# First loads in another order, fourteen transposes ahead of the first product, and a last norm made token tile by token tile, in a two-block model on one core

## The chip, the cores and the metric

One of the cores of a Trainium2 chip runs the whole program. The metric is the device time of one execution in microseconds. Five engines run beside each other, each through a queue of its own in order: TensorE (PE, with its weight loads as PEld), VectorE (DVE), ScalarE (ACT), GpSimd (POOL) and SyncE (SP), which here only issues transfers.

## The reference

`x` holds 256 tokens of 1024 channels. Three kinds of stages follow each other, all with a residual: feed-forwards, an even mixer (convolution and banded attention), an odd mixer (dilated attention and pooling) and two mixers of a second block. The change touches the first feed-forward, the last feed-forward and the last norm:

```python
def rms_norm(x, g):
    y = x * rsqrt(mean(x * x, axis=-1, keepdims=True) + EPS)
    return y * g
def swiglu(x, w_gate, w_up, w_down):
    return (silu(x @ w_gate) * (x @ w_up)) @ w_down

x = x + 0.5 * swiglu(rms_norm(x, g[0]), ffn_w_gate[0, 0], ...)     # first stage, 2752 hidden channels
...
x = x + swiglu(rms_norm(x, ffn_norm_g_2[1]), w_ffn_gate_2[1], ...) # last stage, 2816 hidden channels
return rms_norm(x, final_norm_g_2)
```

## The kernel before

The residual stream `xs` stays in SBUF as two token tiles `t` of 128 tokens by 1024 channels. Weights arrive in units of 128x1024 fp32 (512 KB), listed in `plan` in the order in which they are used. SyncE loads unit `u` into the stage `u % 6`; ScalarE's `split` copies it, rounded, to `whi[u % 4]`; VectorE's `split` writes the rest, `wlo = stage - whi`. TensorE then makes every fp32 product from two or three products of such halves (`three`). The unit's `whi`/`wlo` are free once TensorE has signalled `("used", u)`, four units back.

All queues are written out by hand. `Count` gives each step a semaphore and a value: `K.at(step)` waits for a step, `K.now(name)` for the last increment of one's own. `Banks` hands out the eight PSUM banks, and `room` waits until the bank's earlier user has been read.

A feed-forward stage `g` begins with `norm_T`: TensorE transposes `xs` in eight column blocks `k` (line 590; blocks 0 to 3 need the first half of `x`, 4 to 7 the second). ScalarE writes the high half `hTh` times the norm's column of gains `gcol` (line 1186), VectorE the low half `hTl` (line 1634). The gains come from ten rows in `grow`, transposed by TensorE (line 1156, 128x10 results) and copied by ScalarE (line 1601). The factor 1/rms of a token is applied later: ScalarE sums squares (`square`, line 1197), VectorE scales them (`mean_square`, line 1647), GpSimd takes the power -0.5 (line 2405), and TensorE spreads it over the columns (`row`, line 598). Then `wide_tiles` makes pairs of a 128x512 and a 128x256 product (lines 628, 629): a unit has four blocks `k` and two output tiles, so eight pairs. Those of a unit wait for `("lo", u)` and for `hTl` of each block.

The stage ends with `down`: 22 rows of `w_down`, one unit each, accumulate in four banks, (token tile t, channel half n), with three 128x512 products for each bank and row (lines 580 to 582). So every row writes all four banks, twelve products, and all four are complete at the very end. VectorE then adds each bank to `xs` (`residual`, line 1671).

After the last stage, `g = 9`, come the sums of squares of both token tiles on ScalarE, `mean_square(10)`, `norm(10)` on GpSimd, two 128x1024 passes of VectorE that write `fin` (lines 2396 and 1634; `fin` lies over stages 0 and 1, the gains `gfin` in stage 2), and two output transfers of 512 KB from ScalarE's queue (line 1609).

At the start, SyncE's queue has the first half of `x`, the small constants (among them `ident`), the second half of `x`, units 0 to 3, more constants, and so on; ScalarE's queue has three small loads of `grow`, then the splits of units 0 and 1, then the gains and `norm_T`, and then the two splits that are due (`side.due`).

## Time and profile before

| | us |
|---|---|
| median of 3 runs | 1850.64 |
| lowest and highest | 1850.51, 1861.02 |
| the profiled execution | 1855.39 |
| its span in the trace | 1853.6 |
| TensorE busy in it | 1808.7 |

The span runs from the first to the last thing in the trace; the profiled execution takes 1.8 us more than it. Rows of a timeline give the start in us from the span's start, the duration, the engine and line, and in brackets the idle time ahead with what ended it.

### The profile page before, as it was taken

Reading aid. Unit: us, or ns where it says so; the run is one execution under the profiler, and the core shown is the slowest. Engines: PE = TensorE matmul, PEld = TensorE weight load, DVE = VectorE, ACT = ScalarE, POOL = GpSimd, SP = SyncE. Lnnn points to the kernel's source line nnn. Section 1 sums busy time; section 2 is a strip of 40 time slices with the busy share of each in tenths; the row PEclk is TensorE's granted clock in tenths of the full one; section 3 lists DMA queues with packets and bytes.
Section 4 is the critical chain, followed back from the end, with each engine's and each line's share of the span. In section 5 each row is a group of like instructions: output and inputs, shape, how many; then the busy total and the mean of one; then the engine's idle time right before and its main releaser. Section 6 shows DMA issues by size and latency. Waiting matters only on the chain.

```text
span 1853.6 us, 24863 instructions
## 1 busy us (share of the span) xinstructions
PE 1808.7 (98%) x9690; PEld 1524.0 (82%) x9690; DVE 1278.3 (69%) x1931; ACT 946.4 (51%) x1341; POOL 30.6 (2%) x36
## 2 busy tenths in 40 slices
PE   8999999999999999999999999999999999999998
PEld 6888877888788878788888787888888778888886
DVE  6775795776477646577746867767755778667763
ACT  5554654555455535465535545555544544555542
POOL 0000000000000001000000000000000000000000
PEclk9999998999999999999999999999999999999999
DMA  7666522666566655356665544556655553466662
GB/s 241 191 180 193 170 80 68 183 188 193 176 182 183 193 181 166 93 177 192 185 193 174 159 119 136 163 176 188 189 189 170 143 155 118 148 182 191 183 191 93
DMA packets 227471, 309.25 MB, mean 167 GB/s; under 512 B 22479, under 2 KB 176239, under 8 KB 227355
## 3 DMA queue, kind: packets, MB, share of 16 engines
q1 hardware_dynamic: 227046, 306.57, 54.6%
q8 instruction: 78, 1.28, 0.3%
q10 hardware_dynamic: 308, 1.09, 0.1%
q14 instruction: 39, 0.31, 0.0%
HBM read 306.57 MB, written 1.05 MB: 166 GB/s over the span
## 4 chain that ended last, share of the span: by engine, by line
PE 76%; issue 11%; DVE 8%; ACT 3%; DMA 1%; SPq 0%; DVEq 0%; POOLq 0%; POOL 0%; ACTq 0%
PE ps L628 21%; PE ps L580 13%; PE ps L581 13%; PE ps L582 13%; PE ps L629 10%; DVE wlo L1625 2%; ACT whi L1175 1%; PE ps L1085 1%; PE ps L763 1%; DVE ev_acc L1634 1%; DVE m_scr L2201 1%; DVE m_scr L1634 1%; PE ps L590 1%; PE ps L789 1%; PE ps L776 1%
## 5 line engine op out<-in xcount | busy, mean ns | idle before, releaser
L1625 DVE TENSOR_TENSOR wlo<-staging,whi 128x1024 fp32r<-128x1024 f32 (+2 forms) x582 | 698.7, 1210 | 401.3 <-ACT whi L1175 400.8
L1175 ACT ACTIVATE whi<-staging 128x1024 fp32r<-128x1024 f32 (+2 forms) x582 | 608.4, 1049 | 522.0 <-PE ps L582 318.8
L628 PE MATMUL ps<-hT,whi 128*128 128x512 f32 x1984 | 702.5, 399 | 2.7 <-DVE hT L1634 2.7
L629 PE MATMUL ps<-hT,wlo 128*128 128x256 f32 x1984 | 558.6, 282 | 0.0
L628 PEld LDWEIGHTS ps<-hT,whi 128*128 128x128 f32 x1984 | 374.2, 189 | 94.2 <-DVE hT L1634 3.8
L629 PEld LDWEIGHTS ps<-hT,wlo 128*128 128x128 f32 x1984 | 376.9, 190 | 0.0
L580 PE MATMUL ps<-whi,fh 128*128 128x512 f32 (+1 forms) x528 | 209.6, 397 | 0.0
L581 PE MATMUL ps<-wlo,fh 128*128 128x512 f32 (+1 forms) x528 | 209.6, 397 | 0.0
L582 PE MATMUL ps<-whi,fl 128*128 128x512 f32 (+1 forms) x528 | 209.1, 396 | 0.0
L580 PE MATMUL ps<-whi,hT 128*128 128x512 f32 (+3 forms) x464 | 184.9, 399 | 1.8 <-issue 1.4
L582 PE MATMUL ps<-whi,hT 128*128 128x512 f32 (+3 forms) x464 | 177.6, 383 | 0.0
L581 PE MATMUL ps<-wlo,hT 128*128 128x512 f32 (+3 forms) x464 | 177.4, 382 | 0.0
L580 PEld LDWEIGHTS ps<-whi,fh 128*128 128x128 f32 (+1 forms) x528 | 99.5, 188 | 25.5 <-DVE wlo L1625 1.5
L582 PEld LDWEIGHTS ps<-whi,fl 128*128 128x128 f32 (+1 forms) x528 | 99.5, 188 | 24.0
L581 PEld LDWEIGHTS ps<-wlo,fh 128*128 128x128 f32 (+1 forms) x528 | 99.5, 188 | 23.4
L580 PEld LDWEIGHTS ps<-whi,hT 128*128 128x128 f32 x464 | 87.3, 188 | 23.0 <-issue 5.0
L582 PEld LDWEIGHTS ps<-whi,hT 128*128 128x128 f32 x464 | 87.2, 188 | 16.2
L581 PEld LDWEIGHTS ps<-wlo,hT 128*128 128x128 f32 x464 | 87.5, 189 | 14.2 <-issue 0.5
L1244 ACT ACTIVATE fh<-sg 128x512 fp32r<-128x512 f32 x62 | 39.2, 633 | 113.8 <-DVE sg L1725 113.8
L1710 DVE TENSOR_TENSOR sg<-sg,R 128x512 f32<-128x512 f32 x124 | 85.8, 692 | 4.3
L1707 DVE TENSOR_TENSOR sg<-ps,sg 128x512 f32<-128x512 f32 x124 | 84.8, 684 | 0.2
L580 PE MATMUL ps<-hT,whi 128*128 128x256 f32 x288 | 82.9, 288 | 0.0
(319 smaller groups left out, 1883.1 us busy)
## 6 DMA issues: line engine op xcount, KB each, us to landing
staging<-in_w_in SPq DMA_DIRECT2D x92, 512.0 KB, 3.5
staging<-in_ffn_w_down SPq DMA_DIRECT2D x88, 512.0 KB, 4.2
staging<-in_ffn_w_gate SPq DMA_DIRECT2D x84, 512.0 KB, 4.1
staging<-in_ffn_w_up SPq DMA_DIRECT2D x84, 512.0 KB, 4.5
staging<-in_w_ffn_gate SPq DMA_DIRECT2D x44, 512.0 KB, 3.9
staging<-in_w_ffn_up SPq DMA_DIRECT2D x44, 512.0 KB, 4.5
staging<-in_w_ffn_down SPq DMA_DIRECT2D x44, 512.0 KB, 3.5
staging<-in_od_w_in SPq DMA_DIRECT2D x16, 512.0 KB, 4.2
```

What stands on the lines that cost most here:

```text
L580: e.matmul(o, lh, rh, start=start, stop=False)
L581: e.matmul(o, lh, rl, start=False, stop=False)
L582: return e.matmul(o, ll, rh, start=False, stop=stop)
L590: w = e.transpose(ps[:, t * 128:t * 128 + 128], xs[:, t, k * 128:k * 128 + 128], ident)
L628: e.matmul(o, wh[:, kk, sl], hT[:, k, :], start=k == 0, stop=False)
L629: m = e.matmul(o[:, 0:256], wl[:, kk, sl], hTh[:, k, :], start=False, stop=k == KD - 1)
L1175: e.activation(whi[u % NH][:, 0:n], stage[u % NS][:, 0:n], ACT.Copy).then_inc(*K.inc("hi", ("hi", u)))
L1244: e.activation(f.fh[:, 2 * p:2 * p + 2, :], s[:, :, 0:256], ACT.Copy).then_inc(*K.inc("fh", ("fh", g, p, 0)))
L1625: e.tensor_tensor(wlo[u % NH][:, 0:n], stage[u % NS][:, 0:n], whi[u % NH][:, 0:n].bitcast(F32), ALU.subtract).then_inc(*K.inc("lo", ("lo", ...
L1634: return e.scalar_tensor_tensor(out=o, in0=a, scalar=scalar, in1=b, op0=f1, op1=f2)
L1707: e.tensor_tensor(ss, PS[:, b:b + 2, 0:256], ss, ALU.add).then_inc(*K.inc("ps_r", *[("ev", u) for u in users]))
L1710: e.tensor_tensor(ss, ss, R22, ALU.mult).then_inc(*K.inc("ps_r", ("scaled", g, p, part)))
```

## The change

It has three parts.

1. **First loads.** SyncE's queue now begins with the small constants, then the first half of `x`, unit 0, the second half of `x`, unit 1. ScalarE and VectorE no longer split units 0 and 1 ahead of everything: they make blocks 0 to 3 of `hTh` and `hTl`, then split unit 0, then blocks 4 to 7, then units 1 to 3.
2. **Fourteen transposes.** Before the first product of the first stage TensorE transposes `ident` fourteen times into the bank that this product then starts afresh.
3. **The end.** The last four rows of the last `down` are done bank by bank: all twelve products of (t 0, n 0), then those of (0, 1), (1, 0) and (1, 1). VectorE's `finish` adds and normalises token tile 0 ahead of tile 1. The squares of tile 1 are summed in two halves of 512 channels, its mean is put together by two small instructions, its root is a GpSimd instruction of its own, and its result is written in two halves. Tile 0 and the first half of tile 1 go out from SyncE's queue, the second half from ScalarE's.

```diff
@@ tensor_program: down, ffn
-            def down(g, rows):
+            def down(g, rows, ahead=0):
...
-                for k, (h, lo, sl, step) in enumerate(rows):
+                for k, (h, lo, sl, step) in enumerate(rows[0:len(rows) - ahead]):
...
-                        wide_tiles(g, room_pair(*users), (part, g, p))
+                        ps = room_pair(*users)
+                        if g == 0 and p == 0 and part == "gate":
+
+                            for _ in range(14):
+                                e.transpose(ps[0][:, 0:128], ident, ident)
+                        wide_tiles(g, ps, (part, g, p))
...
-                for _ in down(g, f.rows):
+                if f is not f5:
+                    for _ in down(g, f.rows):
+                        pass
+                    return
+
+                for _ in down(g, f.rows, ahead=4):
                     pass
+                us = {}
+                for t in range(2):
+                    ts = slice(t * 128, t * 128 + 128)
+                    for n in range(2):
+                        cols_n = slice(n * 512, n * 512 + 512)
+                        for k in range(f.nf - 4, f.nf):
+                            h, lo, sl, step = f.rows[k]
+                            if k not in us:
+                                us[k] = unit()
+                                e.wait_ge(*K.at(*step))
+                            u, wh, wl = us[k]
+                            w = three(bk("dn", g, t, n), h[sl, ts], lo[sl, ts], wh[sl, cols_n], wl[sl, cols_n], False,
+                                      k == f.nf - 1)
+                        w.then_inc(*K.inc("prod", ("dn", g, t, n)))
+                        done("dn", g, t, n)
@@ scalar_program
             def norm_T(f):
                 g = f.g
                 for k in range(KD):
+                    if g == 0 and k == 4:
+                        split()
...
-            split()
-            split()
-            side.due += 2
+            side.due += 3
...
-            square(10)
-            for t in range(2):
-                e.wait_ge(*K.at("final", t))
-                e.dma_start(out[0].rearrange("(t p) d -> p t d", p=128)[:, t, :], fin[:, t, :]).then_inc(
-                    *K.dma("out", *([("out",)] if t else [])))
+
+            for t, n, o in ((0, 2, 0), (1, 1, 1), (1, 2, 8)):
+                a = 512 * n - (512 if t else 1024)
+                e.wait_ge(*K.at("x", 9, t, n - 1))
+                if o:
+                    e.wait_ge(*K.now("sq"))
+                e.activation(junk[:, a:512 * n], xs[:, t, a:512 * n], ACT.Square,
+                             accum_out=st8[:, o:o + 1]).then_inc(*K.inc("sq", ("sq", 10, o)))
+            e.wait_ge(*K.at("final", 2))
+            e.dma_start(outv[:, 1, 512:1024], fin[:, 1, 512:1024]).then_inc(*K.dma("out", ("out",)))
             e.wait_ge(*K.at("out"))
+            e.wait_ge(*K.at("out", 1))
@@ vector_program (norm_T and the first splits change as on ScalarE)
+            def finish():
+
+                g = f5.g
+                for n in range(2):
+                    residual(g, f5.coef, 0, n)
+                e.wait_ge(*K.at("sq", 10, 0))
+                e.tensor_scalar(st8[:, 2:3], st8[:, 0:1], 1.0 / D, EPS, ALU.mult, ALU.add).then_inc(
+                    *K.inc("ms", ("ms", 10, 0)))
+                e.wait_ge(*K.at("rstd", 10, 0))
+                e.wait_ge(*K.at("gfin"))
+                stt(fin[:, 0, :], xs[:, 0, :], st8[:, 4:5], gfin, ALU.mult, ALU.mult).then_inc(
+                    *K.inc("final", ("final", 0)))
+                for n in range(2):
+                    residual(g, f5.coef, 1, n)
+                e.wait_ge(*K.at("sq", 10, 1))
+                e.tensor_scalar(st8[:, 9:10], st8[:, 1:2], 1.0 / D, EPS, ALU.mult, ALU.add).then_inc(*K.inc("ms"))
+                e.wait_ge(*K.now("ms"))
+                e.wait_ge(*K.at("sq", 10, 8))
+                stt(st8[:, 3:4], st8[:, 8:9], 1.0 / D, st8[:, 9:10], ALU.mult, ALU.add).then_inc(
+                    *K.inc("ms", ("ms", 10, 1)))
+                e.wait_ge(*K.at("rstd", 10, 1))
+                for n in range(2):
+                    sl = slice(512 * n, 512 * n + 512)
+                    stt(fin[:, 1, sl], xs[:, 1, sl], st8[:, 5:6], gfin[:, sl], ALU.mult, ALU.mult).then_inc(
+                        *K.inc("final", ("final", 1 + n)))
@@ gpsimd_program
-            norm(10)
+            for t in range(2):
+                e.wait_ge(*K.at("ms", 10, t))
+                root(st8[:, 4 + t:5 + t], st8[:, 2 + t:3 + t], 1, ("rstd", 10, t))
@@ sync_program
+            e.dma_start(cst[:, 0:KEEP], A["consts"][:, 0:KEEP]).then_inc(*K.dma("consts", ("consts",)))
             for n in range(2):
                 e.dma_start(xs[:, :, n * 512:n * 512 + 512], xv[:, :, n * 512:n * 512 + 512]).then_inc(
                     *K.dma(f"x_in{n}", ("x", -1, 0, n), ("x", -1, 1, n)))
-                if n == 0:
-                    e.dma_start(cst[:, 0:KEEP], A["consts"][:, 0:KEEP]).then_inc(*K.dma("consts", ("consts",)))
-            for u in range(4):
+                unit(n)
+            for u in range(2, 4):
                 unit(u)
...
+            e.wait_ge(*K.at("final", 0))
+            e.dma_start(outv[:, 0, :], fin[:, 0, :]).then_inc(*K.dma("out_sp"))
+            e.wait_ge(*K.at("final", 1))
+            e.dma_start(outv[:, 1, 0:512], fin[:, 1, 0:512]).then_inc(*K.dma("out_sp", ("out", 1)))
```

The order of ScalarE's instructions at the start, before; `whi` is a split, `gcol` the gains, `hT` the high halves of `norm_T`:

```order
4 L1175 ACT_TABLE_LOAD
5 L1175 ACTIVATE whi<-staging 128x1024 [waits s_st0]
6 L1175 ACTIVATE whi<-staging 128x1024 [waits s_st1]
7 L1601 ACTIVATE gcol<-ps 128x8x10 [waits s_hT]
8 L1186 ACTIVATE hT<-ps,gcol 128x256 [waits s_nT,s_gcol]
9 L1186 ACTIVATE hT<-ps,gcol 128x256 [waits s_nT] x7
```

And in the changed kernel:

```order
4 L1628 ACT_TABLE_LOAD
5 L1628 ACTIVATE gcol<-ps 128x8x10 [waits s_hT]
6 L1215 ACTIVATE hT<-ps,gcol 128x256 [waits s_nT,s_gcol]
7 L1215 ACTIVATE hT<-ps,gcol 128x256 [waits s_nT] x3
8 L1202 ACTIVATE whi<-staging 128x1024 [waits s_st0]
9 L1215 ACTIVATE hT<-ps,gcol 128x256 [waits s_nT] x4
10 L1202 ACTIVATE whi<-staging 128x1024 [waits s_st1]
11 L1202 ACTIVATE whi<-staging 128x1024 [waits s_st2]
12 L1202 ACTIVATE whi<-staging 128x1024 [waits s_st3]
```

The two splits have moved from ahead of the gains to between and behind the blocks of `hT`; VectorE's queue changes in the same places. TensorE's first instructions, before:

```order
3 L590 MATMUL ps<-cst,xs 128x128 [waits s_x_in0]
4 L590 MATMUL ps<-cst,xs 128x128 x7
5 L590 MATMUL ps<-cst,xs 128x128 [waits s_x_in1]
6 L590 MATMUL ps<-cst,xs 128x128 x5
7 L590 MATMUL ps<-cst,xs 128x128 [waits s_gcol]
8 L590 MATMUL ps<-cst,xs 128x128
9 L628 MATMUL ps<-hT,whi 128x512 [waits s_lo,s_hTl]
10 L629 MATMUL ps<-hT,wlo 128x256
```

And in the changed kernel, where line 591 is the transposes of `xs` and 723 the new ones of `ident`:

```order
3 L591 MATMUL ps<-cst,xs 128x128 [waits s_x_in0]
4 L591 MATMUL ps<-cst,xs 128x128 x7
5 L591 MATMUL ps<-cst,xs 128x128 [waits s_x_in1]
6 L591 MATMUL ps<-cst,xs 128x128 x5
7 L591 MATMUL ps<-cst,xs 128x128 [waits s_gcol]
8 L591 MATMUL ps<-cst,xs 128x128
9 L723 MATMUL ps<-cst 128x128 [waits s_hTl]
10 L723 MATMUL ps<-cst 128x128 x13
11 L629 MATMUL ps<-hT,whi 128x512 [waits s_hTl,s_lo]
12 L630 MATMUL ps<-hT,wlo 128x256
```

The fourteen stand between the transposes of `xs` and the first wide product, and wait for `hTl` of the blocks that had the bank. VectorE's last instructions, before; `xs<-ps,xs` is a residual, `staging` holds `fin`:

```order
1388 L1625 TENSOR_TENSOR wlo<-staging,whi 128x1024 [waits s_hi] x16
1389 L1671 TENSOR_TENSOR xs<-ps,xs 128x512 [waits s_prod] x4
1390 L1647 TENSOR_SCALAR st<-st 128x2 [waits s_sq]
1391 L1634 SCALAR_TENSOR_TENSOR staging<-xs,st,staging 128x1024 [waits s_gfin,s_pow]
1392 L1634 SCALAR_TENSOR_TENSOR staging<-xs,st,staging 128x1024
```

And in the changed kernel:

```order
1389 L1658 TENSOR_TENSOR wlo<-staging,whi 128x1024 [waits s_hi] x16
1390 L1706 TENSOR_TENSOR xs<-ps,xs 128x512 [waits s_prod] x2
1391 L1801 TENSOR_SCALAR st<-st 128x1 [waits s_sq]
1392 L1667 SCALAR_TENSOR_TENSOR staging<-xs,st,staging 128x1024 [waits s_gfin,s_pow]
1393 L1706 TENSOR_TENSOR xs<-ps,xs 128x512 [waits s_prod] x2
1394 L1810 TENSOR_SCALAR st<-st 128x1 [waits s_sq]
1395 L1667 SCALAR_TENSOR_TENSOR st<-st 128x1 [waits s_sq,s_ms]
1396 L1667 SCALAR_TENSOR_TENSOR staging<-xs,st,staging 128x512 [waits s_pow]
1397 L1667 SCALAR_TENSOR_TENSOR staging<-xs,st,staging 128x512
```

Token tile 0 is finished, with its 128x1024 pass, ahead of the residuals of tile 1.

## Rows read from the trace of the kernel before

**Rows 1.** The page, part 1: busy time, share of the span and instructions of each engine.

```profile
PE 1808.7 (98%) x9690; PEld 1524.0 (82%) x9690; DVE 1278.3 (69%) x1931; ACT 946.4 (51%) x1341; POOL 30.6 (2%) x36
```

**Rows 2.** The timeline of SyncE, start: issue start, us, what is loaded.

```profile
0.74 0.44 SPq L2514 DMA_DIRECT2D xs<-in_x  x1
...
2.31 1.02 SPq L2509 DMA_DIRECT2D staging<-in_ffn_w_gate  x2
3.37 1.22 SPq L2509 DMA_DIRECT2D staging<-in_ffn_w_up  x2
```

**Rows 3.** The DMA view of 2.3 to 2.7 and 3.3 to 3.7 us: median us to landing.

```profile
staging<-in_ffn_w_gate SPq DMA_DIRECT2D x1, 512.0 KB, 6.5
...
staging<-in_ffn_w_up SPq DMA_DIRECT2D x1, 512.0 KB, 8.5
```

**Rows 4.** The timeline of TensorE, 5 to 14.5 us: start, us, what.

```profile
5.69 0.99 PE L1156 MATMUL ps<-cst,grow 10*128 10x10 f32 x8 [5.69 <-DMA grow<-in_ffn_norm_g]
6.61 3.25 PE L590 MATMUL ps<-cst,xs 128*128 128x128 f32 x14
...
13.98 0.77 PE L628 MATMUL ps<-hT,whi 128*128 128x512 f32 x1 [1.67 <-DVE hT L1634]
```

**Rows 5.** The timeline of ScalarE, 8 to 24 us.

```profile
8.88 1.06 ACT L1175 ACTIVATE whi<-staging 128x1024 fp32r<-128x1024 f32 x1 [5.65 <-DMA staging<-in_ffn_w_gate]
...
11.35 0.22 ACT L1601 ACTIVATE gcol<-ps 128x80 f32<-128x80 f32 x1
11.61 3.02 ACT L1186 ACTIVATE hT<-ps,gcol 128x256 fp32r<-128x256 f32 x8
```

**Rows 6.** The timeline of VectorE, 8 to 24 us.

```profile
12.62 3.22 DVE L1634 SCALAR_TENSOR_TENSOR hT<-ps,gcol,hT 128x256 fp32r<-128x256 f32 x8
```

**Rows 7.** The timeline of TensorE around 16 and around 20.5 us.

```profile
16.04 0.63 PE L628 MATMUL ps<-hT,whi 128*128 128x512 f32 x1
...
16.68 0.63 PE L628 MATMUL ps<-hT,whi 128*128 128x512 f32 x1
...
20.32 0.40 PE L628 MATMUL ps<-hT,whi 128*128 128x512 f32 x1
...
20.68 0.40 PE L628 MATMUL ps<-hT,whi 128*128 128x512 f32 x1
```

**Rows 8.** TensorE at 297 us, and windows: PE, PEld, DVE, ACT, POOL busy, granted clock.

```profile
297.12 0.63 PE L581 MATMUL ps<-wlo,ev_mh 128*128 128x512 f32 x1
...
289.00:299.00 10.00, 10.00 (x36) 8.94 (x37) 2.02 (x5) 2.48 (x3) 0.69 (x1) 0.50 0.00 0
```

**Rows 9.** The timeline of 1832.9 to 1836 us, and the last product.

```profile
1834.38 1.23 DVE L1625 TENSOR_TENSOR wlo<-staging,whi 128x1024 fp32r<-128x1024 f32 x1 [1.59 <-ACT whi L1175]
...
1835.14 0.40 PE L580 MATMUL ps<-whi,fh 128*128 128x512 f32 x1
...
1844.04 0.40 PE L582 MATMUL ps<-whi,fl 128*128 128x512 f32 x1
```

**Rows 10.** The timelines of ScalarE, VectorE and GpSimd behind the last product.

```profile
1845.73 1.06 ACT L1197 ACTIVATE junk<-xs 128x1024 bf16<-128x1024 f32 x1
...
1849.21 1.57 ACTq L1609 DMA_DIRECT2D out<-staging  x2
...
1846.92 0.17 DVE L1647 TENSOR_SCALAR st<-st 128x2 f32<-128x2 f32 x1 [1.75 <-ACT junk L1197]
1847.89 2.48 DVE L1634 SCALAR_TENSOR_TENSOR staging<-xs,st,staging 128x1024 f32<-128x1024 f32 x2 [0.81 <-POOL st L2405]
...
1847.16 0.69 POOL L2405 TENSOR_TENSOR st<-st,phalf 128x2 f32<-128x2 f32 x1 [183.67 <-DVE st L1647]
```

**Rows 11.** The DMA view of 1849 to 1854 us.

```profile
out<-staging ACTq DMA_DIRECT2D x2, 512.0 KB, 2.7
```

**Rows 12.** Groups by line with shapes kept apart: count | busy us, mean ns | idle before.

```profile
L1244 ACT ACTIVATE fh<-sg 128x512 fp32r<-128x512 f32 x62 | 39.2, 633 | 113.8 <-DVE sg L1725 113.8
...
L1710 DVE TENSOR_TENSOR sg<-sg,R 128x512 f32<-128x512 f32 x124 | 85.8, 692 | 4.3
```

16 lines of the change are left out of this document (7 added, 9 removed).

## The prediction, made before the changed kernel was run

> **What bounds the kernel now.** I read the page's busy times first: TensorE is busy for 1808.7 of 1853.6 us [rows 1]. Between the first and the last wide product the change touches no instruction, so the question is only how much time lies ahead of TensorE's stream and behind it. Hence the timelines of the two ends.
>
> At the start the first wide product begins at 13.98 us [rows 4]. TensorE had the gains' products at 5.69 and the transposes of x from 6.61 to 9.86. It was ScalarE that was late: in its queue the gains stand behind two splits, the first of which waited until 8.88 for its unit, so that the gains were copied at 11.35 and `hTh` began at 11.61 [rows 5]. The `lo` halves followed from 12.62 [rows 6], and the product waited for the first of them.
>
> From 13.98 the pace is half of what it becomes. A pair (512 and 256 columns) takes 16.68 - 16.04 = 0.64 us, later 20.68 - 20.32 = 0.36 us; a 512-column product lasts 0.63 us against 0.40 [rows 7]. At 297 us the same length, 0.63, goes with a granted clock of 0.50, which is the 1.2 GHz level [rows 8]; so the start runs at 1.2 GHz too, and 0.40 us belongs to 2.4 GHz. The fast pace comes at about 19.3 us, 5.3 us after the first wide product. The price of that stretch is 5.3 x (1 - 0.36/0.64) = 2.3 us.
>
> At the end the last product starts at 1844.04 and lasts 0.40 us [rows 9]. The other 1853.6 - 1844.44 = 9.2 us are squares, mean, root, two passes and two stores in a chain [rows 10].
>
> **Part 1, the first loads.** ScalarE's two splits ahead of the gains are gone from that place. The gains need only TensorE's products (5.69 + 0.99 = 6.68), so they are copied at about 6.7 instead of 11.35. The blocks of `hTh` then follow the transposes, which come 0.43 us apart (two of 0.217: fourteen took 3.25, of which the last one's own length, 0.42, is not a step, 2.83/13 [rows 4]): blocks 0 to 3 are done by 9.1. Unit 0, no longer behind the second half of x, has landed before that: it stood at 2.31 + 6.5 = 8.8 [rows 2, 3] with 512 KB more ahead of it, and 512 KB are worth (11.9 - 8.8)/2 = 1.5 us (unit 0 to unit 2, 3.37 + 8.5 [rows 2, 3]), so about 7.3. Its split takes ScalarE from 9.1 to 10.2 (1.06 us [rows 5]) and VectorE to 11.4 (1.23 us [rows 9]). The first product could start at 11.5, 2.5 us earlier than now.
>
> The second half of x takes unit 0's old place in the stream, with the same bytes ahead of it, so it lands at about 8.7. Without it TensorE stands still after eight transposes, at 6.61 + 8 x 0.217 = 8.35; the price is 0.35 us. Its other eight run from 8.7 to 10.4. Blocks 4 to 7 on ScalarE (0.38 us each, 3.02/8 [rows 5]) now stand behind unit 0's split, and unit 1's splits behind them: ScalarE 10.2 to 11.7 and 12.8, VectorE with 0.40 us a block [rows 6] to 13.0 and 14.3. Unit 1 is needed eight pairs, 2.9 to 5.1 us, after the first wide product, so that wait hides while TensorE starts at 11.8 or later. The queue of SyncE issues no more bytes than before, and units 4 and on land as now. The three splits that are due, the squares and the root are needed by `row` only after four units.
>
> **Part 2, the fourteen transposes.** They stand in TensorE's queue ahead of the product that could start at 11.5. At the present pace they take 14 x 0.217 = 3.0 us, from 10.4 to 13.5. So the first wide product comes at 13.5 instead of 13.98, and four fifths of what part 1 gained is spent, unless the transposes raise the clock. Do they? The trace has one test: from 5.69 to 9.86 TensorE was busy without a gap, 0.99 us with the small products and 3.25 with fourteen transposes, and the pace did not rise until 5.3 us of wide products had passed [rows 4, 7]. That speaks for no, though weakly, since the small products stand in it and 1.8 us of idling follow. I take it: the pace rises 5.3 us after the first wide product as before, and the start gains 0.5 us. The bounds: 0.3 (x lands later, at 8.9) and 0.8 (no pause for it), and the case in which they do count, below.
>
> The Trainium skill has a rule on this. Its page "TensorE: Matmul & The Clock Gate", section "Part 4: PE-mode transpose", says that transposes do not count as activity in the way products do, so that the full clock is not reached by them. That rule speaks against this part, and the stretch of 5.69 to 9.86 us agrees with it. By it the sum of the start is the 0.5 us that the rows gave.
>
> **Part 3, the end.** The last 48 products keep their number and pace, (1844.04 - 1835.14)/38 = 0.234 us, so they start at 1833.03. But the last unit is now needed after nine of them, at 1835.14, not after 36. VectorE finishes its `lo` at 1834.38 + 1.23 = 1835.61 [rows 9], since its buffer is freed only by the row before the four. TensorE stalls 0.5 us, once, and its last product ends at 1844.95. Nobody else waits in that stall.
>
> Token tile 0 is complete at 1839.3. Two residuals (0.69 each), its squares (1.06 + 0.19), mean 0.17, root 0.69 and pass 1.24 [rows 10, 12] end by 1843.8, the first residual of tile 1 by 1844.5, all beside TensorE. VectorE is thus free 0.5 us before the last bank is complete; if that margin went, each further 0.1 us would be on the path.
>
> Behind the last product, with gaps of 0.03 to 0.07 as now: residual 0.69; squares of 512 channels 0.73 (now 1.06 and the read-out to 1846.89, 1.16 in all, less 0.43, since a 128x512 pass of ScalarE takes 0.63 [rows 10, 12]); mean 0.17; root 0.69; two passes of 0.69 [rows 12], where a whole one took 1.24 [rows 10]. That is 3.66 and 0.25 of gaps: the last half is ready at 1848.86. Its store of 256 KB: 512 KB took 2.7 from issue to landing [rows 11], and half the bytes are 0.77 less by the rate above, or nothing less; I take 0.6 less, 2.1, nearer to the rate, as stores of both queues overlap. After the last landing the span goes on for about 0.5 (the second issue at 1850.4, 2.7, then 1853.6). End: 1848.9 + 2.1 + 0.5 = 1851.5, a gain of 2.1 us. Bounds: 1.4 (2.7 for the half store, 0.1 more of stall) to 2.5 (no stall).
>
> **Sum.** 0.5 + 2.1 = 2.6 us. Against the profiled execution's own 1855.39 (span 1853.6 and 1.8 outside it) that is 1852.8; against the median of 1850.64, **1848.0 us**. The profiled execution lay 4.7 us above that median and one timed run 10 above it, so the scatter of runs is larger than the gain. A measurement of this kernel can tell about 1%, 18.5 us, from no change; both ends together are 13.98 + 9.2 = 23 us, most of it untouched, so nothing here can leave that band.
>
> **Rivals.**
> *The transposes do raise the clock.* For: from 9.86 to 13.98 TensorE was idle most of the time, so the earlier activity may have been lost, not ignored; in the changed kernel TensorE is busy from 5.69 with one gap of 0.2. Then the rise falls inside the fourteen, which end between 12.1 (all of them at the faster pace, 0.36/0.64 of 0.217 each) and 13.5; take 12.6. The start gains 1.4 us by position and the 2.3 us of slow products: 3.7, with the end 5.8, so 1844.8. In the best case (12.1, and 2.5 at the end) it is 1844.0. Against: the stretch to 9.86 us. The Trainium skill's page of the same name, section "What's actually happening", says that activity releases the throttle, without setting transposes aside there; by that sentence this case would be the one.
>
> *The start is lost and more: slower.* The second half of x is now fourth in the stream, among weights in pieces of 1 KB. If it lands late, eight transposes, the fourteen and every product shift with it, since the fourteen cannot start before. With x at 8.7 the first wide product is at 13.5; the end's 2.1 us are used up when it is at 16.1, that is from a landing at 11.3 on. If it landed where unit 2 did, at 11.9, it is 16.7: 2.7 lost, 2.1 gained, 1851.2. Against: SyncE's loads so far landed in the order of issue, 8.8 and 11.9 [rows 3].
>
> *The end gives little.* If VectorE reaches the last residuals late, because tile 0's squares, root and pass stand ahead of them in its queue, and the half passes cost 0.69 each, the end gains 0.5 or so, with the start 1.0: 1849.6. The point is the margin of 0.5 us above.
>
> **How the numbers follow.** Forecast as above, 52%; the clock is raised, 30%; little at the end, 11%; slower, 7%. The likeliest gives 1848.0. The range takes in the raised clock down to 1844 and, upwards, the forecast against the higher profiled execution, 1852.8, where the other two cases lie as well: 1844 to 1853. Faster by over 1% has 1%, slower by over 1% has 1%, within 1% has 98%.
>
> **What would show it.** In the changed profile: gains copied by 7 us; the second half of x at about 8.7; fourteen transposes 0.22 us apart ending near 13.5 (0.12 apart at their end if the clock rises in them); the first wide product at 13.5 and pairs of 0.64 until 19; one gap of 0.5 us at TensorE nine products into the last 48; 6.6 us from the last product to the end instead of 9.2. I would be wrong above all if the transposes wake the clock, or if runs of the two kernels differ by their scatter of some us.

## The result, and the profile of the changed kernel

The changed kernel took 1846.96 us (median of 20 runs), the kernel before 1853.68 us (median of 20). The ratio on record is 0.9967, with a 95% interval of 0.9955 to 0.998. That is 6.1 us less, with 3.7 and 8.3 as the ends of the interval; the two medians taken by themselves differ by 6.7. The profiled executions differ by 8.3 us: 1855.39 with a span of 1853.6 before, 1847.09 with a span of 1845.3 after.

The timeline of TensorE at the start of the changed kernel (start, us, what, xcount, idle before and its releaser), which answers to [rows 4, 7]:

```profile
5.46 1.00 PE L1183 MATMUL ps<-cst,grow 10*128 10x10 f32 x8 [5.46 <-DMA grow<-in_ffn_norm_g]
6.39 1.97 PE L591 MATMUL ps<-cst,xs 128*128 128x128 f32 x8
8.64 1.97 PE L591 MATMUL ps<-cst,xs 128*128 128x128 f32 x8 [0.28 <-DMA xs<-in_x]
10.41 1.91 PE L723 MATMUL ps<-cst 128*128 128x128 f32 x14
12.07 0.47 PE L629 MATMUL ps<-hT,whi 128*128 128x512 f32 x1
12.39 0.28 PE L630 MATMUL ps<-hT,wlo 128*128 128x256 f32 x1
12.50 0.40 PE L629 MATMUL ps<-hT,whi 128*128 128x512 f32 x1
```

And ScalarE in the same stretch, which answers to [rows 5]:

```profile
6.50 0.24 ACT L1628 ACTIVATE gcol<-ps 128x80 f32<-128x80 f32 x1 [3.31 <-PE ps L1183]
7.18 1.69 ACT L1215 ACTIVATE hT<-ps,gcol 128x256 fp32r<-128x256 f32 x4 [0.45 <-PE ps L591]
8.77 1.05 ACT L1202 ACTIVATE whi<-staging 128x1024 fp32r<-128x1024 f32 x1
9.72 1.56 ACT L1215 ACTIVATE hT<-ps,gcol 128x256 fp32r<-128x256 f32 x4
```

The gains are copied at 6.50, blocks 0 to 3 of `hTh` are through by 8.87, and unit 0's split begins at 8.77, as soon as they are. The second half of x releases TensorE at 8.64, after a pause of 0.28. Then the reader should see one number: sixteen transposes of x go in steps of 0.22 (eight take 1.97 with the last one's own 0.42 in it), but the fourteen start at 10.41 and the wide product behind them at 12.07, which is 0.12 each on average. The first pair of wide products takes 12.50 - 12.07 = 0.43 us and its 512-column product lasts 0.47. Before, the first one lasted 0.77, and later pairs took 0.64 [rows 4, 7]. So TensorE is at the fast pace before any wide product has run.

The end, in the timelines of TensorE, VectorE, ScalarE, GpSimd and the two queues, which answer to [rows 9, 10]:

```profile
1829.55 0.50 PE L581 MATMUL ps<-whi,fh 128*128 128x512 f32 x1 [0.37 <-DVE wlo L1658]
1829.89 0.39 PE L582 MATMUL ps<-wlo,fh 128*128 128x512 f32 x1
...
1838.55 0.40 PE L583 MATMUL ps<-whi,fl 128*128 128x512 f32 x1
```

```profile
1836.09 1.28 DVE L1667 SCALAR_TENSOR_TENSOR staging<-xs,st,staging 128x1024 f32<-128x1024 f32 x1 [0.66 <-POOL st L2461]
1837.29 0.68 DVE L1706 TENSOR_TENSOR xs<-ps,xs 128x512 f32<-128x512 f32 x1
1838.98 0.69 DVE L1706 TENSOR_TENSOR xs<-ps,xs 128x512 f32<-128x512 f32 x1 [1.01 <-PE ps L583]
1839.59 0.14 DVE L1810 TENSOR_SCALAR st<-st 128x1 f32<-128x1 f32 x1
1840.54 0.16 DVE L1667 SCALAR_TENSOR_TENSOR st<-st 128x1 f32<-128x1 f32 x1 [0.80 <-ACT junk L1639]
1841.37 1.41 DVE L1667 SCALAR_TENSOR_TENSOR staging<-xs,st,staging 128x512 f32<-128x512 f32 x2 [0.67 <-POOL st L2461]
```

```profile
1839.71 0.63 ACT L1639 ACTIVATE junk<-xs 128x512 bf16<-128x512 f32 x1 [0.98 <-DVE xs L1706]
1840.24 0.19 ACT L1639 ACTIVATION_READ_ACCUMULATOR junk<-xs 128x1 f32 x1
1842.81 0.38 ACTq L1642 DMA_DIRECT2D out<-staging  x1
```

```profile
1840.78 0.55 POOL L2461 TENSOR_TENSOR st<-st,phalf 128x1 f32<-128x1 f32 x1 [4.72 <-DVE st L1667]
```

The last 48 products start at 1826.92. The tenth waits: it begins 0.75 us after the ninth and the next follows after 0.34, where the step is 0.234, so the stall costs 0.62. The last product ends at 1838.95, and 6.35 us later the span is over, against 9.16 before. The DMA view of the last stretch (KB each, median us to landing):

```profile
out<-staging SPq DMA_DIRECT2D x1, 256.0 KB, 2.1
out<-staging ACTq DMA_DIRECT2D x1, 256.0 KB, 2.1
```

Each of the two stores, now 256 KB, has landed 2.1 us after its issue (2.7 for 512 KB [rows 11]).

**Where the time went.** I cut each execution at two points that any change of the ends leaves in place: the start of `row`'s product in the first feed-forward, and the end of the last product. The first piece is the start, the last the end, and the piece between, the same instructions in all kernels but for the order of the last 48 products, I call the middle. All numbers are us and come from the timeline of TensorE; the moment from which the pace is fast is where the trace records the granted clock rising to 1.00, and the steps shorten at the same place. (Ahead of its first record the windows view prints 1.00 as well, though the steps there are the slow ones, so at the very start the steps are what to read.) The end is the span, rounded to 0.1, less the end of the last product, and so is exact to 0.05 only. The middle contains the stall of 0.62 us where there is one.

| execution | first wide product | fast pace from | `row`'s product | middle | end | span |
|---|---|---|---|---|---|---|
| before | 13.98 | 19.3 | 27.75 | 1816.69 | 9.16 | 1853.6 |
| before, once more | 14.86 | 19.1 | 27.97 | 1821.38 | 9.15 | 1858.5 |
| changed | 12.07 | 10.8 | 23.26 | 1815.69 | 6.35 | 1845.3 |
| changed, once more | 12.63 | 12.1 | 24.01 | 1813.61 | 6.38 | 1844.0 |
| no fourteen transposes | 11.39 | 14.6 | 24.04 | 1818.70 | 6.36 | 1849.1 |
| the same, once more | 11.49 | 15.5 | 24.52 | 1819.96 | 6.32 | 1850.8 |
| start alone | 13.32 | 12.7 | 24.51 | 1818.18 | 9.11 | 1851.8 |
| end alone | 13.87 | 10.5, then 17.4 | 26.61 | 1815.37 | 6.32 | 1848.3 |
| fourteen products instead | 14.49 | 12.0 | 25.67 | 1809.40 | 6.33 | 1841.4 |
| old order of loads | 11.85 | 11.0 | 23.16 | 1808.27 | 6.37 | 1837.8 |
| ten transposes at the head | 11.52 | 10.1 | 22.70 | 1818.43 | 6.37 | 1847.5 |
| the same, with a new end | 11.40 | 10.3 | 22.78 | 1812.29 | 6.33 | 1841.4 |
| three rows bank by bank | 13.36 | 13.2 | 24.54 | 1819.53 | 6.83 | 1850.9 |
| ten and ten, and a new end | 12.95 | 13.0 | 24.14 | 1822.45 | 6.31 | 1852.9 |

The start gains 27.75 - 23.26 = 4.5 us between the two profiled executions, and 27.86 - 23.64 = 4.2 between the means of two each. The end gains 2.8 less the stall of 0.62, 2.2. Together that is 6.4 to 6.7 us, and the timed ratio says 6.1. The remaining 1.6 us of the 8.3 is the middle without the stall (1.0 with it). The middle varies by 14 us over the table, although nothing was changed in it but the order of the last products; what it consists of is told at the end.

### The profile page after: what moved, and what is told of

Read it like the earlier page. It is cut to its first block, busy times and chain, and to the rows that moved or that the text cites. A ratio compares the mean times of both kernels' runs of the same rounds, so it can differ in the third digit from the quotient of the medians.

```text
span 1845.3 us, 24901 instructions
## 1 busy us (share of the span) xinstructions
PE 1804.6 (98%) x9704; PEld 1523.9 (83%) x9704; DVE 1277.0 (69%) x1934; ACT 946.7 (51%) x1343; POOL 31.0 (2%) x37
## 4 chain that ended last, share of the span: by engine, by line
PE 86%; DVE 8%; ACT 3%; issue 2%; DMA 1%; SPq 0%; DVEq 0%; POOLq 0%; POOL 0%; ACTq 0%
PE ps L629 25%; PE ps L581 14%; PE ps L582 14%; PE ps L583 14%; PE ps L630 13%; DVE wlo L1658 2%; ACT whi L1202 1%; PE ps L1112 1%; PE ps L790 1%; DVE ev_acc L1667 1%; PE ps L591 1%; DVE m_scr L2265 1%; DVE m_scr L1667 1%; PE ps L816 1%; DVE m_scr L2263 1%
## 5 line engine op out<-in xcount | busy, mean ns | idle before, releaser
L629 PE MATMUL ps<-hT,whi 128*128 128x512 f32 x1984 | 694.1, 394 | 1.1 <-DVE hT L1667 1.1
L582 PEld LDWEIGHTS ps<-wlo,hT 128*128 128x128 f32 x464 | 88.2, 190 | 14.6 <-issue 0.5
```

The costliest lines, as they stand in the source:

```text
L582: e.matmul(o, lh, rl, start=False, stop=False)
L629: e.matmul(o, wh[:, kk, sl], hT[:, k, :], start=k == 0, stop=False)
```

## The experiments

Twelve runs were made, of nine new kernels and three kernels once more. Where no ratio is given, the run was one profiled execution.

**The fourteen transposes left out.** Only the loop goes:

```diff
-                        if g == 0 and p == 0 and part == "gate":
-                            for _ in range(14):
-                                e.transpose(ps[0][:, 0:128], ident, ident)
```

> The changed kernel without its fourteen transposes of ident, all else as in it. Theory 1 (the fourteen wake the clock: in the changed kernel the pace rose inside them, the first wide product came at 12.07 us at full pace): without them the first wide product comes when unit 0's low half is ready, 11.1 us, but pairs take 0.64 us for some 5.3 us more, to about 16.4; against the changed kernel 1.0 us is won by position and 2.3 lost by pace, so about 1.3 us longer, 1.0006 to 1.001 of it, and against the kernel before about 4.8 us shorter, 0.9974. Theory 2 (the sixteen transposes of x, now followed by work at once instead of 4 us of idling, are enough): pairs take 0.36 us within a microsecond of 11.1, and the kernel is about 1.0 us shorter than the changed one, 0.9960 of the one before.

Measured: 1850.95 us against 1853.76, a ratio of 0.9989 (0.9977 to 1.0002). Theory 1's 0.9974 lies just outside that interval; what this means is taken up in the account below. The timeline of TensorE:

```profile
8.99 1.97 PE L591 MATMUL ps<-cst,xs 128*128 128x128 f32 x8 [0.58 <-DMA xs<-in_x]
11.39 0.76 PE L629 MATMUL ps<-hT,whi 128*128 128x512 f32 x1 [0.42 <-DVE wlo L1654]
...
12.16 0.63 PE L629 MATMUL ps<-hT,whi 128*128 128x512 f32 x1
...
12.80 0.63 PE L629 MATMUL ps<-hT,whi 128*128 128x512 f32 x1
...
14.68 0.39 PE L629 MATMUL ps<-hT,whi 128*128 128x512 f32 x1
...
15.03 0.39 PE L629 MATMUL ps<-hT,whi 128*128 128x512 f32 x1
```

The first wide product comes at 11.39, 0.1 from the 11.5 that my working had for "could start". But its pairs take 0.64, up to 14.6. Compared with the kernel before the slow stretch is already shorter, 3.2 us for 5.3, though nothing was added ahead of it: TensorE waits 0.42 us ahead of its first wide product, where it did little from 9.86 to 13.98 [rows 4].

A second execution of the same kernel, later:

> The changed kernel without the fourteen transposes once more. Theory A (the sixteen transposes of x alone can raise the clock, and the instant of the rise varies): the rise falls anywhere from 10 to 15 us; where it falls before 11.4, the product of row begins at 22.5, where it falls at 14.6 as in the first execution, at 24.0. Theory B (the fourteen are needed for the clock): slow pairs of 0.64 until 14.5 or later again, and the product of row at 24.0 or later.

Measured: the fast pace from 15.5, slow for 4.0 us, `row`'s product at 24.52. That is theory B as far as two executions go: in both, the first pairs behind the sixteen transposes of x are slow (TensorE paused for 0.58 and 0.81 us between the halves of x, and for 0.42 and 0.19 ahead of the first product). Theory A's case of an early rise did not show.

**The start alone**, with the old end: `mean_square(10)`, `norm(10)` and the two stores of 512 KB from ScalarE's queue stand again behind four rows in the old order.

```diff
-                if f is f5:
-                    finish()
-                    return
...
-            for t, n, o in ((0, 2, 0), (1, 1, 1), (1, 2, 8)):
...
+            square(10)
+            for t in range(2):
+                e.wait_ge(*K.at("final", t))
+                e.dma_start(outv[:, t, :], fin[:, t, :]).then_inc(
+                    *K.dma("out", *([("out",)] if t else [])))
```

> The changed kernel with the end of the one before: last rows row by row, one norm for both tiles, two stores of 512 KB. If the ends are worth what the two traces say (last product to end 9.2 us before, 6.35 after, and a stall of 0.45 paid for it), this keeps a start worth about 4.2 us (first wide product at 12.1 and no slow pairs): ratio to the kernel before 0.9977, last product to end 9.2 us again, no stall in the last 48 products. If instead the gain at the start is handed back later (a queue that was ahead waits again), the ratio is 1.000.

Measured: 1851.78 us, 0.9985 (0.9971 to 1.0) of the kernel before. In its trace the last rows of the gains landed late and TensorE began at 6.72 instead of 5.46; the fourteen took from 11.11 to 13.32, 0.158 each, and the pairs behind them ran at the fast pace. `row`'s product is at 24.51, 3.2 to 3.5 us ahead of the kernel before; the end is 9.11.

**The end alone**, with the old loads, both splits ahead of the gains and no fourteen.

```diff
-                    if g == 0 and k == 4:
-                        split()
...
-            side.due += 3
+            split()
+            split()
+            side.due += 2
```

> The kernel before with only the new end. Expected: first wide product at 14.0 us and pairs of 0.64 to about 19.3 as before, one stall of about 0.45 us in the last 48 products, 6.4 us from the last product to the end: 2.3 us shorter than the kernel before, ratio 0.9988. If the new end works only because something ahead moved, it gives nothing: 1.000.

Measured: 1852.00 us, 0.9998 (0.9983 to 1.0013). The end takes 6.32 with the stall, so the local reading is a gain of 2.2 us; the timed ratio does not show it, and its interval allows a loss of 2.4 us or a gain of 3.2. What makes this run valuable is its start, which is the old one. TensorE, and the windows view of 13.95 to 17.36 us (PE, PEld, DVE, ACT, POOL busy, granted clock, DMA):

```profile
6.77 3.25 PE L591 MATMUL ps<-cst,xs 128*128 128x128 f32 x14
11.52 0.44 PE L591 MATMUL ps<-cst,xs 128*128 128x128 f32 x2 [1.50 <-ACT gcol L1624]
13.87 0.69 PE L629 MATMUL ps<-hT,whi 128*128 128x512 f32 x1 [1.92 <-DVE hT L1663]
...
14.58 0.63 PE L629 MATMUL ps<-hT,whi 128*128 128x512 f32 x1
```

```profile
13.95:17.36 3.41, 3.41 (x11) 2.92 (x12) 3.41 (x7) 3.41 (x6) 0.00 (x0) 0.50 1.10 349
```

Two transposes of x were left for 11.52. They take 0.44 together. In the kernel before, the same two take 0.69 in both executions:

```profile
11.63 0.69 PE L590 MATMUL ps<-cst,xs 128*128 128x128 f32 x2 [1.76 <-ACT gcol L1601]
```

```profile
12.50 0.69 PE L590 MATMUL ps<-cst,xs 128*128 128x128 f32 x2 [2.69 <-ACT gcol L1601]
```

So at 11.5 us the pace was fast, after nothing but the gains' eight small instructions, which are transposes too, and fourteen transposes of x. The rise is recorded at 10.5, half a microsecond after TensorE had stopped at 10.02. From there to 13.87 TensorE did these 0.44 us of work and nothing else: it idled for 1.50 us ahead of them and for 1.92 behind. From 13.95 to 17.36 the granted clock is 0.50, the 1.2 GHz level. Transposes had raised the clock, and it was lost again behind the two idle stretches. This is one of three executions with the old start; in the other two, the kernel before, the same two transposes took 0.69 us, so there the rise had not come by then.

**Fourteen products in the place of the fourteen transposes**, on the same block and into the same bank:

```diff
-                                e.transpose(ps[0][:, 0:128], ident, ident)
+                                e.matmul(ps[0][:, 0:128], ident, ident, start=True, stop=True)
```

> The changed kernel with fourteen ordinary 128x128 fp32 products of ident by ident in place of its fourteen transposes (the same result, which nobody reads). If transposes count for the clock as products do, the rise comes at the same place and the first wide product at about 12.1 us. If transposes count for less, the rise comes earlier here than in the changed kernel, at least not later, and each product's step is as long as a transpose's (0.22 us slow, 0.12 fast).

```profile
10.92 3.82 PE L723 MATMUL ps<-cst 128*128 128x128 f32 x28
14.49 0.47 PE L629 MATMUL ps<-hT,whi 128*128 128x512 f32 x1
```

A product on float32 words stands as two instructions in the trace, so the fourteen are 28 and end later. The fast pace comes at 12.0, as it does with transposes (10.8 to 13.2): the kind of operation makes no difference that shows in this one execution, where the moment varies by 2 us anyway, but the doubled number costs 2 us, `row`'s product being at 25.67.

**The old order of loads**, all else as in the changed kernel: both halves of x and the constants ahead of unit 0.

```diff
-            e.dma_start(cst[:, 0:KEEP], A["consts"][:, 0:KEEP]).then_inc(*K.dma("consts", ("consts",)))
             for n in range(2):
                 e.dma_start(xs[:, :, n * 512:n * 512 + 512], xv[:, :, n * 512:n * 512 + 512]).then_inc(
                     *K.dma(f"x_in{n}", ("x", -1, 0, n), ("x", -1, 1, n)))
-                unit(n)
-            for u in range(2, 4):
+                if n == 0:
+                    e.dma_start(cst[:, 0:KEEP], A["consts"][:, 0:KEEP]).then_inc(*K.dma("consts", ("consts",)))
+            for u in range(4):
```

> The changed kernel with the old order of loads: both halves of x and the constants ahead of the weights. Theory A (the new order of loads is worth what unit 0 comes earlier, 1.5 us, less the 0.3 us pause): unit 0 lands at 8.5 to 8.8 instead of 7.0, so that the hi half of unit 0 begins at 8.9 and not 8.8: ScalarE would have had blocks 0 to 3 of hTh done by then only, the pause of TensorE is gone, and the start is within 0.2 us of the changed kernel's (product of row 23.2 to 24.5 by the instant of the rise). Theory B (the order of loads is what lets the gains be copied early): the constants land later than 4 us, the gains are copied after 7.5 and the first wide product comes 1 us or more later.

```profile
6.39 3.68 PE L591 MATMUL ps<-cst,xs 128*128 128x128 f32 x16
9.86 2.24 PE L723 MATMUL ps<-cst 128*128 128x128 f32 x14
11.85 0.47 PE L629 MATMUL ps<-hT,whi 128*128 128x512 f32 x1
```

```profile
9.32 1.06 ACT L1202 ACTIVATE whi<-staging 128x1024 fp32r<-128x1024 f32 x1 [0.46 <-DMA staging<-in_ffn_w_gate]
```

In the changed kernel unit 0 was issued at 1.65 and landed 5.3 us later (its DMA view):

```profile
staging<-in_ffn_w_gate SPq DMA_DIRECT2D x1, 512.0 KB, 5.3
```

Here its split begins at 9.32, when it lands; there it had landed by 7.0, but ScalarE was not free for it before 8.77. So 0.55 us of the 2.3 count at ScalarE, and against them the pause of 0.28 at TensorE is gone: its sixteen transposes run without a gap and end 0.5 us earlier. `row`'s product is at 23.16 against 23.26 and 24.01. VectorE has unit 0's `lo` half ready at 11.64, against 11.07 in the changed kernel, and both times that is before the fourteen transposes end. So `row`'s product lies where theory A put it (23.2 to 24.5), and of the start the order of loads is worth nothing that shows in this one execution. What is left to carry the start is the order of ScalarE's work (the gains copied first, blocks 0 to 3, then unit 0's split); no run changes that alone.

**Ten transposes at the head of TensorE's queue**, waiting for the constants alone, and none ahead of the first wide product:

```diff
             e.wait_ge(*K.at("consts"))
-            e.wait_ge(*K.at("grow"))
             ps = room(("gcol",))
+            for _ in range(10):
+                e.transpose(ps[:, 128:256], ident, ident)
+            e.wait_ge(*K.at("grow"))
```

> The changed kernel without the fourteen transposes ahead of the first wide product; ten transposes of the same block stand instead at the head of TensorE's queue, ahead of the gains' products, and wait for the constants alone (landing at about 3.1 us). Theory A (any work raises the clock, transposes too, and the earlier TensorE is busy the earlier it rises): the ten run from about 3.2 to 5.4 us in steps of 0.22, the clock rises before 10.8 us, so that the last of x's transposes go in steps of 0.12; TensorE then waits 1 to 1.5 us for the lo half of unit 0, the first wide product begins at 11.0 to 11.4 and its pairs take 0.36 at once; the product of row begins at about 22.5 us, 0.8 before the changed kernel. Theory B (what counts is that TensorE is busy right up to the first wide product): the wait of 1 to 1.5 us loses the clock, and the first pairs take 0.64 as without the fourteen; the product of row begins at about 24.0. Theory C (transposes of the constants count less than those of x): as B.

```profile
3.29 2.40 PE L1178 MATMUL ps<-cst 128*128 128x128 f32 x10 [3.29 <-DMA cst<-in_consts]
...
8.96 1.65 PE L591 MATMUL ps<-cst,xs 128*128 128x128 f32 x8 [0.42 <-DMA xs<-in_x]
11.52 0.47 PE L629 MATMUL ps<-hT,whi 128*128 128x512 f32 x1 [0.91 <-DVE wlo L1656]
...
11.94 0.39 PE L629 MATMUL ps<-hT,whi 128*128 128x512 f32 x1
```

The fast pace comes at 10.1, in the middle of x's transposes; TensorE then waits 0.91 us for unit 0's `lo` half and still starts at the fast pace, so an idle stretch of 0.9 did not lose it, where in the end alone 1.5 and 1.9, with 0.44 of work between, did. With no transposes between, the first product is 0.5 to 1.1 us earlier than in the changed kernel, and `row`'s product comes at 22.70, 0.6 to 1.3 earlier. Theory A gave 22.5.

**Three rows bank by bank instead of four:**

```diff
-                for _ in down(g, f.rows, ahead=4):
+                for _ in down(g, f.rows, ahead=3):
...
-                        for k in range(f.nf - 4, f.nf):
+                        for k in range(f.nf - 3, f.nf):
```

> The changed kernel with three rows of the last feed-forward finished bank by bank instead of four. Theory A (the stall of 0.4 to 0.5 us comes from the buffer that the row before the banks frees): that row is now one earlier against the first need, since 12 products of a row (2.8 us) go before the banks and the last unit is needed after six products, so the stall is gone. What is won comes back at VectorE: tile 0 is complete 4.2 us before the end instead of 5.6, its pass of 1.3 us ends 0.4 us later than tile 1's first bank asks, and the last residual starts up to 0.4 us late. Span from the start of the last 48 products to the end 18.0 to 18.5 us, as the changed kernel's 18.4. Theory B (the stall comes from VectorE's splits themselves, late whatever the order): the stall stays at 0.4 to 0.5 us and the end is 0.4 us longer than the changed kernel's.

```profile
1842.61 1.28 DVE L1667 SCALAR_TENSOR_TENSOR staging<-xs,st,staging 128x1024 f32<-128x1024 f32 x1 [0.66 <-POOL st L2461]
1843.81 1.28 DVE L1706 TENSOR_TENSOR xs<-ps,xs 128x512 f32<-128x512 f32 x2
```

The last 48 products start at 1832.66 and end at 1844.07: 11.41 us where the changed kernel needs 12.03. That is 47 x 0.234 + 0.40, no stall. The end is 6.83 instead of 6.35, and the rows say why: tile 0's pass ends at 1843.89, tile 1's two residuals run back to back behind it (x2, no idle time named), and the second, whose bank was complete at 1844.07, begins 0.4 us late. From the start of the 48 to the end it is 18.24 against 18.38. Theory A held, with both of its halves.

**Both repairs together.** At the end VectorE now also takes tile 1's first residual ahead of its pass over tile 0; at the start ten transposes stand at the head and ten in the place of the fourteen.

```diff
+                residual(g, f5.coef, 1, 0)
                 e.wait_ge(*K.at("rstd", 10, 0))
...
-                for n in range(2):
-                    residual(g, f5.coef, 1, n)
+                residual(g, f5.coef, 1, 1)
```

> The changed kernel with three edits: ten transposes of the constants at the head of TensorE's queue, ten instead of fourteen ahead of the first wide product, and at the end three rows bank by bank, with VectorE's residual of tile 1's first half ahead of its pass over tile 0. Theory A (the clock rises the earlier TensorE is busy): full pace from about 8.5 us on, the ten take 1.2 us from 9.8 and hide in the wait for unit 0's lo half, the first wide product begins at 11.0 to 11.4 at full pace, the product of row at 22.5 (0.8 before the changed kernel); no stall at the end and 6.3 us behind the last product, 0.45 less. Span 1.2 us under the changed kernel's: 1844.1, timed ratio to the changed kernel 0.9993. Theory B (activity before 5 us counts for nothing): the first wide product at 11.9 and the start as in the changed kernel; 0.45 us less in all. Either is near the limit of what the runs can tell, so the trace decides.

```profile
1844.51 0.69 DVE L1708 TENSOR_TENSOR xs<-ps,xs 128x512 f32<-128x512 f32 x1
1845.13 1.28 DVE L1669 SCALAR_TENSOR_TENSOR staging<-xs,st,staging 128x1024 f32<-128x1024 f32 x1
1846.62 0.69 DVE L1708 TENSOR_TENSOR xs<-ps,xs 128x512 f32<-128x512 f32 x1 [0.21 <-PE ps L583]
```

The end does what was meant: no stall (11.41 us for the 48), the last residual 0.03 behind its bank, 6.31 us to the end, so 0.6 better than the changed kernel. The start refutes theory A: TensorE was busy from 3.03 on, with pauses of 0.50 and 0.35, and the fast pace came at 13.0, later than in four of the five executions with fourteen transposes and none at the head. Theory B's 11.9 is missed too, by 1.1. Timed: 1850.20 against 1855.31, 0.9967 (0.9954 to 0.998).

**The new end with the other start**, ten transposes at the head and none behind (the edits of the two kernels above, no others):

> The changed kernel with ten transposes of the constants at the head of TensorE's queue, none ahead of the first wide product, and the end of the version with three rows and VectorE's exchanged order. Theory A (the instant of the rise varies by itself): the first wide product at 11.1 to 11.6, since no transposes stand before it; the product of row at 22.3 to 22.8 where the rise comes by 11 us, and at 24.0 where it comes at 14; no stall and 6.3 us at the end. Span 0.45 us under the changed kernel's for the end, and 1.3 under to 0.5 over for the start. Theory B (the ten at the head bring the rise forward for certain): rise by 10.5 us, product of row at 22.7 as in the first execution of such a start. Timed against the kernel before, 0.995 to 0.997 either way.

Measured: fast pace from 10.3, first wide product at 11.40 after 0.94 us of waiting, `row`'s product at 22.78, no stall, an end of 6.33. The start is 0.9 us better than the mean of the changed kernel's two, within 0.1 of the other execution with such a start, and the end with its stall is 0.6 us better. The timed ratio is 0.9974 (0.9961 to 0.9987), which does not tell this kernel from the changed one. That the ten at the head bring the rise forward is not settled: it came at 10.1 and 10.3 with them, at 13.0 with them and a pause of 0.50 for the gains behind them, and at 10.5 in the end alone, without them.

**The changed kernel and the kernel before once more.**

> The changed kernel itself once more, for its scatter and as the neighbour of the other runs. Theory A (the 8.3 us between the two profiled executions are 6.8 us of the two ends and the rest scatter of the stages between): first wide product at 12.0 to 12.1, product of row at 23.2 to 23.4, last 48 products with one stall of 0.4 to 0.5, 6.3 to 6.4 us behind the last product, all within 0.1 us of the first execution, while the stretch between moves by up to 3 us; timed ratio to the kernel before 0.9955 to 0.998. Theory B (the ends themselves vary, the early clock rise was luck): the rise comes at another time, and the first wide product's pairs take 0.64 in some execution.

Measured: 1847.27 us against 1855.31, a ratio of 0.9959 (0.9946 to 0.9972). The end repeats to 0.03 us, the stall exactly. The start does not: the fast pace comes at 12.1, within the fourteen again but near their end, and the first wide product at 12.63. So theory A's figure for the start was too narrow by 0.6, and B's "early clock rise was luck" is half true: that it comes before the first wide product held in all five executions with fourteen transposes there, when it comes varies by 2 us.

> The kernel before once more, as a second base for the parts of the time. Theory A (the clock rises at an instant of its own once TensorE has been busy for some us, and the idle stretch from 9.9 to 14.0 us is what put it off): first wide product at 14.0 to 14.4, its pairs 0.64 and slow for 2 to 6 us, the product of row at 26.5 to 28.0; 9.1 to 9.2 us from the last product's end to the end. Theory B (the first execution's 19.3 us was exact and hangs on the wide products alone): slow for 5.2 to 5.4 us again, the product of row at 27.7 to 28.1.

Measured: the fast pace from 19.1, `row`'s product at 27.97, an end of 9.15. The two theories are not told apart well: the slow stretch lasted 4.2 us this time, so B's 5.3 is missed, but the moment stayed at 19; A's range for `row`'s product holds, its 14.0 to 14.4 for the first wide product (14.86) does not.

## Why the prediction was right, and where it was wrong

The time, 1846.96, lies in the range and 1.0 us under the forecast, and the class, within 1%, held. But the forecast's mechanism was not what happened; the rival's was, and part of the agreement is that it was made from a median of three runs, 1850.64, where 20 runs gave 1853.68. That part is luck: from 1853.68 the same 2.6 us would have forecast 1851.1, 4.1 us too much. What is to be compared is the gain: 2.6 us forecast, 5.8 for the rival, 6.1 timed and 6.4 to 6.7 in the traces.

*Part 1, the first loads: right.* Gains copied at 6.50 (about 6.7), second half of x at 8.64 (8.7), pause 0.28 (0.35), split of unit 0 on ScalarE from 8.77 (9.1), the first product possible at 11.39 (11.5), by the run without the fourteen. The order of loads, to which I gave 1.5 us of unit 0's landing, bought nothing that shows: that landing was hidden behind ScalarE and the fourteen. In other executions of this start the second half of x released TensorE at 8.94 to 9.32, so 8.7 was up to 0.6 us early.

*Part 2, the fourteen transposes: wrong.* The step that failed is "I take it: the pace rises 5.3 us after the first wide product as before, and the start gains 0.5 us". The rise fell inside the fourteen (10.8 and 12.1), which ended at 12.07 and 12.63 and not at 13.5; the rival had taken 12.6 and a gain of 3.7, and 4.2 to 4.5 was measured. The test on which I leaned, TensorE busy from 5.69 to 9.86 with the pace unchanged, could not decide it: in no execution of the table did the rise come before 10.1, and the end alone shows what can follow that stretch, a fast pace at 11.5 which was gone again at 13.95. I had named this loss as the argument for the rival and then weighed it below the stretch itself.

*Transposes and the clock.* In the end alone two transposes take 0.44 us at 11.52 with nothing but transposes before them, and in all five executions with fourteen transposes in that place the pace is fast before the first wide product. The Trainium skill's page "TensorE: Matmul & The Clock Gate" says in "Part 4: PE-mode transpose" that the full clock does not engage for transposes, since they do not count as busy in the same way. These rows contradict it, and they decide. The kernel before and the one without the fourteen, where the rise came only behind wide products, fit that rule but fit a late rise as well. The same page's "What's actually happening", by which activity releases the throttle, agrees with these runs.

*How much the fourteen are worth at the start* is less than the rise suggests. Without them the first wide product is 0.6 to 1.2 us earlier but the pairs slow for 3.2 to 4.0 us: `row`'s product at 24.28 in the mean of two, against 23.64 with them, and 24.54 with them in the kernel with three rows. So by the traces it is 0.6 us at best and not clearly above the scatter of the rise. The larger part of the start, 27.86 - 24.28 = 3.6 us, comes with part 1 alone: 3.0 by position (first wide product at 14.42 and 11.44 in the means), and the rest from a slow stretch of 3.6 us instead of 4.8. That second effect was in neither my forecast nor the rival.

*The timed runs of the parts do not add up to this account.* Without the fourteen, the traces give a gain of 3.6 + 2.2 = 5.8 us over the kernel before, but the timed ratio gives 2.0, with 4.3 as the upper end of its interval. The start alone and the end alone are timed at 2.8 and 0.4 us, 3.2 together, where the whole is timed at 6.1; the intervals of these two are wide enough for that. So the gains at the two ends are shown where they arise, in each trace, and what each part is worth in the whole time is not. By the timed ratios to the kernel before, each timed beside its own runs of it (0.9967 and 0.9959 with the fourteen, 0.9989 without), they would be worth 4 to 6 us, most of which the start does not contain; the middle, told at the end, is large enough to hold it, and whether by chance is open.

*Part 3, the end: right to 0.1 us in sum.* Stall 0.62 at the tenth product (0.5, at the same product), 6.35 behind the last product (6.6), a store of 256 KB in 2.1 (2.1), gain 2.2 (2.1). The margin of VectorE, which I called 0.5 us, shows as the 1.01 us that it waited for the last bank; the kernel with three rows used it up and paid 0.48.

*The rivals.* x did not land late, and the end did not give little. In start alone it was the gains' rows that landed late, on ScalarE's queue, by 1.3 us; I had not named that. It moved every later step of the start.

## What to carry to other kernels

A few microseconds at the head of a kernel are won by ordering the work of the engine that everybody waits for: copying the gains and half of the input ahead of the first split was worth 3.6 us in the traces of the start, the order of the loads nothing that shows. To judge whether a stretch of filler work holds the clock, look at what stands between it and the real work: idle time behind it can hide that it did. A gain seen at one place in a trace is worth that much there; whether the whole time has it is for the timed runs to say, and with a scatter of some us they may not. And where the last products are regrouped so that one output is done early, the operands of all of them are needed early as well: count whose buffer frees the last one, and in which order the engine behind works off what comes free.

## What the runs showed of the hardware that was not expected

**The stages between have two paces.** In each feed-forward the wide products of `gate` and `up` run at one step from beginning to end (in the first, from the rise of the clock on), and this step is one of two: 0.3465 us a pair or 0.353. The same stretch, 510 to 640 us, in the changed kernel and in its second execution (groups by line: count, busy us, mean ns, idle):

```profile
L629 PE MATMUL ps<-hT,whi 128*128 128x512 f32 x296 | 102.8, 392 | 0.0
```

```profile
L629 PE MATMUL ps<-hT,whi 128*128 128x512 f32 x298 | 105.5, 399 | 0.0
```

The mean is 392 ns against 399, TensorE busy without a gap in both, at a granted clock of 1.00 in the windows of both. Some 300 pairs times 0.0066 us are 2.0 us, and stage by stage the executions of the table differ by 0.0 or by 1.9 to 2.1 us, each stage for itself. The product rows of `down` take 0.234 in both. Beside that the mixers differ by up to 3 us each; in them the granted clock is 0.50 for 10 to 27 us in sum, differently in each execution. That is the scatter of the middle, 1808.3 to 1822.5 us. Of the six feed-forwards none and one ran at the slower step in the two executions with the shortest middle (1809.40 and 1808.27), and all six in the one with the longest (1822.45). It was five and five in the kernel before, two and four in the changed kernel, five and six without the fourteen, so this alone could make the differences of some us between their timed runs. What selects the pace, and whether the change has a part in it, I did not find out.

**The moment of the first rise is loose.** In the ten executions in which the fast pace came before the first wide product or with it (in the end alone it was lost again), it came between 10.1 and 13.2 us, with TensorE's first work at 3.0 to 6.7 us. The two are in no order: the pace was fast from 10.1, 10.3 and 13.0 where TensorE began at 3.3, 3.0 and 3.0. What decides it is open.
